# GpSimd normalises the probabilities of mixers A and B, with the scores of A and C two pairs ahead

## What is computed

```python
# A: windowed attention, 8 heads, with a sink logit
s = jnp.where(valid, s + bias, NEG)
p = jax.nn.softmax(jnp.concatenate([s, sink_l], axis=-1), axis=-1)[..., :-1]
o = jnp.einsum('bnkgqj,bnjkd->bnqkgd', p, vb)          # x silu(gate)
# B: latent attention, 4 heads, dense over all positions
s = jnp.einsum('bqhd,bkhd->bhqk', qb, k) * scale
p = jax.nn.softmax(s, axis=-1)
return jnp.einsum('bhqk,bkhd->bqhd', p, v)             # x silu(gate)
# C: 2-D neighbourhood attention, 4 heads
p = jax.nn.softmax(s.reshape(B, C_HEADS, GRID_W, kh * KW), axis=-1)
return layer_norm(DEEPNORM_ALPHA * x + concat([oa, ob, oc]) @ w_out, ln_g, ln_b)
```

## Time and profile before

| | us |
|---|---|
| median of 3 runs | 1917.07 (1913.8 to 1921.44) |
| the profiled execution, as timed | 1914.88 |
| its span, first to last instruction | 1913.1 |
| PE busy | 1821.9 (95%) |
| DVE busy | 940.6 (49%) |
| ACT busy | 786.1 (41%) |
| POOL busy | 467.6 (24%) |

### The profile page before, as it was taken

One profiled execution on the slowest core, in us unless ns is written; L12 is line 12 of the kernel. 1 busy time (PEld: TensorE's weight loads), 2 busy tenths in 40 slices (PEclk: granted clock), 3 DMA queues, 4 the chain that ended last, 5 costly groups with the idle time before them and its releaser, 6 DMA issues.

```text
span 1913.1 us, 32194 instructions
## 1 busy us (share of the span) xinstructions
PE 1821.9 (95%) x12530; PEld 1480.0 (77%) x12530; DVE 940.6 (49%) x2055; ACT 786.1 (41%) x1675; POOL 467.6 (24%) x683
## 2 busy tenths in 40 slices
PE   5999999999999999999999999999999999989996
PEld 3897578889886665889979866888898766578896
DVE  4466655311425765554453475460133277555626
ACT  3445643311225665452233365341212366644512
POOL 3453402311121362001242231140111125500113
PEclk9999999999999998999989999999999999999998
DMA  6865142211125020005146350621212062000312
GB/s 207 251 219 143 36 166 89 84 49 45 45 66 143 15 73 1 1 19 181 56 144 199 88 134 23 209 77 56 67 45 66 22 144 60 26 1 2 110 46 88
DMA packets 148165, 167.16 MB, mean 87 GB/s; under 512 B 18305, under 2 KB 134401, under 8 KB 147505
## 3 DMA queue, kind: packets, MB, share of 16 engines
q1 hardware_dynamic: 146080, 158.75, 27.9%
q0 software_dynamic: 1152, 4.19, 0.6%
q10 hardware_dynamic: 784, 2.16, 0.3%
HBM read 143.00 MB, written 32.65 MB: 92 GB/s over the span
## 4 chain that ended last, share of the span: by engine, by line
PE 88%; DVE 6%; ACT 3%; issue 1%; DMA 1%; POOL 0%; SPq 0%; DVEq 0%; ACTq 0%
PE psum L582 63%; PE psum L703 8%; PE psum L673 8%; PE psum L655 6%; DVE nmax L1056 2%; PE psum L592 1%; PE psum L714 1%; DVE pt_sb L1080 1%; DMA w_stage<-w_out 1%; DVE qB_lo L1217 1%; DMA qA<-x_prompt 0%; ACT w_hi L867 0%; POOL w_lo L473 0%; ACT qB_hi L962 0%; PE psum L568 0%
## 5 line engine op out<-in xcount | busy, mean ns | idle before, releaser
L582 PE MATMUL psum<-w_hi,x_hi 128*128 128x256 f32 (+1 forms) x1344 | 378.5, 282 | 11.5 <-DVE x_lo L1240 6.7
L582 PE MATMUL psum<-w_hi,x_lo 128*128 128x256 f32 (+1 forms) x1344 | 379.0, 282 | 0.0
L582 PE MATMUL psum<-w_lo,x_hi 128*128 128x256 f32 (+1 forms) x1344 | 377.5, 281 | 0.0
L582 PE MATMUL psum<-x_hi,w_hi 128*128 128x512 f32 x816 | 326.6, 400 | 2.4 <-DVE x_lo L1047 1.6
L582 PE MATMUL psum<-x_lo,w_hi 128*128 128x512 f32 x816 | 325.2, 399 | 0.0
L582 PE MATMUL psum<-x_hi,w_lo 128*128 128x512 f32 x816 | 324.9, 398 | 0.0
L473 POOL TENSOR_TENSOR w_lo<-w_stage,w_hi 128x1024 fp32r<-128x1024 f32 (+1 forms) x83 | 164.0, 1985 | 640.6 <-ACT w_hi L867 640.6
L473 DVE TENSOR_TENSOR w_lo<-w_stage,w_hi 128x1024 fp32r<-128x1024 f32 (+1 forms) x77 | 140.2, 1837 | 318.6 <-ACT w_hi L867 318.6
L582 PEld LDWEIGHTS psum<-w_hi,x_hi 128*128 128x128 f32 x1344 | 254.8, 190 | 13.2 <-issue 13.0
L582 PEld LDWEIGHTS psum<-w_lo,x_hi 128*128 128x128 f32 x1344 | 255.2, 190 | 0.2
L582 PEld LDWEIGHTS psum<-w_hi,x_lo 128*128 128x128 f32 x1344 | 253.5, 189 | 0.0
(11 more groups left out here) (141 smaller groups left out, 2678.9 us busy)
## 6 DMA issues: line engine op xcount, KB each, us to landing
w_stage<-w_in SPq DMA_DIRECT2D x48, 512.0 KB, 4.5
w_stage<-w_in SPq DMA_DIRECT2D x88, 256.0 KB, 3.4
toep<-rpb_tile SPq DMA_DIRECT2D x12, 1152.0 KB, 14.6
rpb_tile<-rpb_col SPq DMA_DIRECT2D x48, 192.0 KB
hT<-y SPq DMA_DIRECT2D x18, 512.0 KB, 11.2
y<-hT SPq DMA_DIRECT2D x18, 512.0 KB, 2.7
w_stage<-w_out SPq DMA_DIRECT2D x32, 256.0 KB, 4.2
w_stage<-w_out SPq DMA_DIRECT2D x16, 512.0 KB, 5.1
```

The source lines that it names most:

```text
L582: last = nc.tensor.matmul(out, w, x, start=(n == 0 and part != 1), stop=(n == len(pairs) - 1 and part != 0))
```

## The change

For A and B the group's division behind the values is taken out, and each unit's probabilities are divided ahead of the transpose: DVE takes one reciprocal for each unit (`unit_inverse`), POOL multiplies the probabilities by it in SBUF (`normalise`), in B with 1024 tokens once for each half, and T waits for POOL (`norm_done`) where it waited for ACT (`probs_done`). The gate is then multiplied by the outputs alone. C keeps what it had.

In phase AC the scores run two pairs ahead of T where they ran one pair ahead: PE's order is S of pair j+1, T of pair j-1, R for C, V of pair j-2, and DVE and ACT take the minimum and the exponential of unit i+2 at step i (`LEAD`). There are six probability slots for this, the sixth in a tensor of its own. PE's order in B stays, without R. In DVE's loop `unit_inverse` of unit k-1 stands behind `bound_scores` of unit k; in B, k is i.

```diff
@@ pe_steps
+    if ph == "AC":
+        for j in range(1, n + 2):
+            if EARLY <= 2 * j + 2 < 2 * n:
+                steps += [("S", 2 * j + 2), ("S", 2 * j + 3)]
+            if 0 <= j - 1 < n:
+                steps.append(("T", j - 1, 0))
+            if j - 2 >= 2 and (j - 2) % 2 == 0:
+                steps.append(("R", (j - 2) // 2 - 1))
+            if 0 <= j - 2 < n:
+                steps.append(("V", j - 2))
+        return steps + [("R", n // 2 - 1)]
...
-P_SLOTS = 5
+P_SLOTS = 6
+LEAD = 2
@@ PE, transpose_probs
-                    pe.wait_ge(probs_done, probs_no[s, u])
+                    if u[0] == "C":
+                        pe.wait_ge(probs_done, probs_no[s, u])
+                    else:
+                        pe.wait_ge(norm_done, norm_no[s, u, hf])
@@ PE, spread_sums
+                if units_of(ph, s)[4 * g][0] != "C":
+                    return
@@ ACT
-                        if (EARLY if ph == "AC" else 0) <= i < len(U):
-                            exp_unit(s, i, U[i])
-                act.wait_ge(values_done, s + 1)
+                        k = i + LEAD if ph == "AC" else i
+                        if (EARLY if ph == "AC" else 0) <= k < len(U):
+                            exp_unit(s, k, U[k])
+                wait_full(act, ("O", s, "B", NT - 1))
@@ DVE
+            def unit_inverse(s, u):
+                j = unit_index[s, u]
+                dve.wait_ge(probs_done, probs_no[s, u])
+                nc.vector.reciprocal(rinv[:, j:j + 1], psums[:, j:j + 1]).then_inc(inv_done, 1)
@@ DVE, the loop
-                    for i in range(len(U) + lag - 2):
-                        if (EARLY if ph == "AC" else 0) <= i < len(U):
-                            bound_scores(s, i, U[i])
+                    for i in range(-1 if ph == "AC" else 0, len(U) + lag - 2):
+                        k = i + LEAD if ph == "AC" else i
+                        if (EARLY if ph == "AC" else 0) <= k < len(U):
+                            bound_scores(s, k, U[k])
+                        if 0 <= k - 1 < len(U) and U[k - 1][0] != "C":
+                            unit_inverse(s, U[k - 1])
...
-                        if i >= 5 and (i - 5) % 4 == 0 and i - 5 < len(U):
+                        if i >= 5 and (i - 5) % 4 == 0 and i - 5 < len(U) and U[i - 5][0] == "C":
                             group_rinv(s, ph, (i - 5) // 4)
...
+                        if i >= lag - 2 and (i - lag + 2) % 4 == 0 and i - lag + 2 < len(U) and U[i - lag + 2][0] != "C":
+                            group_out(s, ph, (i - lag + 2) // 4)
@@ POOL
+                def normalise(u, p, hf, n):
+                    j = unit_index[s, u]
+                    pool.wait_ge(inv_done, inv_no[s, u])
+                    cols = slice(512 * hf, 512 * hf + n)
+                    nc.gpsimd.tensor_scalar(p[:, cols], p[:, cols], rinv[:, j:j + 1], None, ALU.mult).then_inc(norm_done, 1)
+
+                for i in range(EARLY):
+                    sink_column(i)
+                for i in range(LEAD, len(U) + 5):
+                    if EARLY <= i < len(U):
+                        (sink_column if U[i][0] == "A" else window_bias)(i)
+                    k = i - LEAD
+                    if 0 <= k < len(U) and U[k][0] == "A":
+                        normalise(U[k], p_slot(k), 0, key_tiles(U[k], s) * P)
...
-                for g in range(len(b_units(s)) // 4):
-                    spread_rinv(s, "B", g)
+                for i, u in enumerate(b_units(s)):
+                    for hf in range(len(halves_of(u, s))):
+                        normalise(u, pB[:, i % 3, :], hf, 512)
```

More of the change, by code:

```diff
@@ L194, in pe_steps @@
             steps.append(("V", j - late))
-    return steps + [("R", n // 2 - 1)]
+    return steps
 def dense_wide(ph, s):
@@ L302, in encoder_kernel, with p_slot @@
         kB_lo = [w[:, 1].rearrange("p k n -> p (k n)").rearrange("p (h n) -> p h n", h=2) for w in (w_hi, w_lo)]
-        pAC = w_stage[:, :, :, :].rearrange("p h k n -> p (h k n)")[:, 0:P_SLOTS * 385].rearrange("p (u n) -> p u n", n=385)
+        pAC = w_stage[:, :, :, :].rearrange("p h k n -> p (h k n)")[:, 0:5 * 385].rearrange("p (u n) -> p u n", n=385)
+        def p_slot(i):
+            return pAC[:, i % P_SLOTS, :] if i % P_SLOTS < 5 else pAC_last[:, :]
         t5_neg = hT[0:A_HEADS, 0, 0:512]
@@ L427, in encoder_kernel @@
         pt_dve_no = Numbered([(s, h) for s in range(RUNS) for ph in PHASES for h in halves(s, ph) if not copied_by_act(s, *h)])
-        group_no = Numbered(all_groups)
+        group_no = Numbered([(s, ph, g) for s, ph, g in all_groups if units_of(ph, s)[4 * g][0] == "C"])
+        inv_no = Numbered([(s, u) for s, u in all_units if u[0] != "C"])
+        norm_no = Numbered([(s, u, hf) for s, u in all_units if u[0] != "C" for hf in range(len(halves_of(u, s)))])
         xh_no = Numbered([("xT", s, t, i) for s in range(RUNS) for t in range(NTILES[s]) for i in range(2)])
@@ L704, in values @@
                                                     pt_sb[:, slot, (c % 4) * P:(c % 4 + 1) * P], start=(c == 0), stop=(c == nk - 1))
-                if ph == "B" and 2 * j + 2 == len(units_of(ph, s)):
-                    last.then_inc(values_done, 1)
+                if pair[0][0] != "C" and j % 2:
+                    last.then_inc(bank_full[b], 1)
             def spread_sums(s, ph, g):
+                if units_of(ph, s)[4 * g][0] != "C":
+                    return
                 b = uses["O", s, ph, g][0]
@@ L1066, in bound_scores @@
                         dve.wait_ge(biasA_loaded[t - 1], 16 * (s + 1))
-                    nc.vector.tensor_tensor_reduce(out=pAC[:, i % P_SLOTS, 0:n], in0=ps[:, 0:n], in1=reversed_keys(biasA[:, t - 1, kv, :] if t else biasA0[:, kv, :], k0, n),
+                    nc.vector.tensor_tensor_reduce(out=p_slot(i)[:, 0:n], in0=ps[:, 0:n], in1=reversed_keys(biasA[:, t - 1, kv, :] if t else biasA0[:, kv, :], k0, n),
                                                    scale=1.0, scalar=nsink[:, A_HEADS * (s // 2) + h:A_HEADS * (s // 2) + h + 1], op0=ALU.add, op1=ALU.min,
@@ L1102, in group_out @@
             def group_out(s, ph, g):
-                dve.wait_ge(gate_scaled, group_no[s, ph, g])
                 key = ("O", s, ph, g)
+                if units_of(ph, s)[4 * g][0] == "C":
+                    dve.wait_ge(gate_scaled, group_no[s, ph, g])
+                else:
+                    wait_full(dve, key)
+                    if g == 0:
+                        dve.wait_ge(silu_done, last_gate(s))
                 dst = gate_slice(s, ph, g)
@@ L1354, in window_bias @@
                                             reversed_keys(toep[:, slot, 3 * (h % 2) + WIN_TYPE[b], :], 0, n), ALU.add).then_inc(biasC_done, 1)
-                for i in range(-2, len(U) + 3):
-                    if i >= 6 and (i - 6) % 4 == 0:
-                        spread_rinv(s, "AC", (i - 6) // 4)
-                    if i + 2 < len(U):
-                        (sink_column if U[i + 2][0] == "A" else window_bias)(i + 2)
+                def normalise(u, p, hf, n):
[11 more added lines that the diff above has]
+                        normalise(U[k], p_slot(k), 0, key_tiles(U[k], s) * P)
+                    if i >= 8 and (i - 8) % 4 == 0 and U[i - 8][0] == "C":
+                        spread_rinv(s, "AC", (i - 8) // 4)
                 for t in range(NT):
```

24 lines of the change are left out of this document (10 added, 14 removed).

## The result

The changed kernel takes 2132.01 us (median of 4 runs, 2123.37 to 2135.11) against 1917.76, a ratio of 1.112 (95% interval 1.110 to 1.115). The profiled execution takes 2129.97 us with a span of 2128.1. The forecast was 1988, with a range of 1970 to 2022.

A forecast was written before the change was run, and what follows sets the result against it. PE was taken to bound every stretch. Costs of 89.4 us (63.6 + 19.3 + 1.7 + 4.8) less gains of 18.1 gave +71.3 us, so 1988 us against 1917.07, 3.7% slower, range 1970 to 2022.

The forecast's parts named there:

- PE's wait in B: Mixer B, T of each pair's second unit: 2.0 us wait with 1024 tokens, 1.38 us with 512.
- the new one has one tensor input and is nearest to the copy: POOL's division in A and B: 0.65 us for 512 columns, 0.50 for 384, 0.40 for 256.
- So PE stays the bound: Mixer A: POOL rises to 47 of 78.6 us, and A gains its 10.6 us but for the head.
- The rival that A gets a new bound: Mixer A: DVE becomes the bound by waiting for ACT, the 10.6 us are not gained, 1999 us; chance 0.05.
- the clock: Rival, mixer B: waits lower PE's clock, 4 us each time, 2028 to 2108 us; chance 0.08.
- the forecast's terms: Mixer B: costs 63.6 + 19.3 + 1.7 less 5.3 and 1.2, on 304.7, make 383 us.
- the wait's links: Mixer B, 1024 tokens: minimum 1.23, reciprocal 0.12, 0.06 to POOL, division 0.65, 0.08 to PE; 2.0 us wait.
- the 0.12 us ahead of DVE's copy: Mixer B, 1024 tokens: a reciprocal between minimum and DVE's copy makes V wait 0.12 us more per pair.
- the lead and the slots: Phase of A and C: the last T of C has its exponential a pair earlier, 0.25 us a run, 1 us gained.
- R worth its 10.6 us: Mixer A: R goes from PE's path for 48 groups at 0.22 us, 10.6 us gained.
- The head of A: Start of mixer A: first reciprocal stands behind the last gate's multiplication, 1.2 us lost in each of four runs, 4.8 us.
- the faster one: Rival, mixer B: the reciprocal comes before the next scores complete, no wait, only the head's loss remains, 1904 us; chance 0.04.

The follow-up runs named there:

- The run with A alone: The changed kernel with mixer B divided as in the kernel before and only mixer A divided on GpSimd: 1942.51 us, ratio 1.016.
- the cheaper form: The changed kernel with GpSimd's division written as a product of two tensors, the reciprocal broadcast along the row: 2038.95 us, ratio 1.065.
- the split: The changed kernel with B divided as before, A's even units on GpSimd, odd on ACT, first four reciprocals ahead of the last gate: 1906.9 us, ratio 0.9957.
- The run with the forecast's own prices: The changed kernel with GpSimd dividing only 144 of each 512 columns in B and 80 in A: 2022.67 us, ratio 1.058.
- the lead alone: The kernel before with only the scores two pairs ahead in A and C and six probability slots, divisions as before: 1911.92 us, ratio 0.9994.

## Why the prediction was wrong, step by step

Direction and place were right: slower, by PE's wait in B for the reciprocal behind the next minimum. The size was a third of the measured one, 71 us where 214 came, and the range ended 110 us short. Three steps made that, some 40, 40 and 69 us by the sums below; the projections, 6 us shorter, take a little back.

The first is the term "the new one has one tensor input and is nearest to the copy", 0.65 us. It was 1.563, and it lay outside the bounds too: the upper one, 1.345, came from a subtraction of two inputs, taken for dearer than anything with one. The runs show the reverse, since the same product written with two inputs takes 1.041. The Trainium skill (GPSIMD Engine Reference, section 3.1) has 0.77 us for 512 columns as a best case; neither form reaches it here, and the measurement decides. In B the term enters 44 times: (1.56 - 0.65) x 44 = 40 us.

The second follows in A, where POOL was put at 47 of 78.6 us, "So PE stays the bound". At 1.2 us for each of 64 divisions it has 75 us and 12 of sink columns, more than the stretch is long. The rival that A gets a new bound was there, but with DVE in the place of GpSimd. The run with A alone shows the loss, 30 us where a gain of some 7 was summed, and the cheaper form and the split, both with PE holding the chain in A again, show whose it is.

The third is the clock, a rival with a chance of 0.08, set against with "here 7 us of work stand around each". The run with the forecast's own prices went to 0.83 and spent 54 us more of PE's busy time at waits of 2.0 us, 37 us of B's length over the forecast's terms; filling the waits gave 46 us of B back in the changed kernel. With the waits at their true length (30 x 2.95, as a pair at the full clock takes 9.96 where it took 7.0; 14 x 2.3, some 3.5 for the last pairs, less 5.3 for R, 119 us) some 69 of B's 188 us remain for the clock; this split is worked out, the 46 are measured. The Trainium skill (TensorE: Matmul & The Clock Gate, HAM oscillation) names waits in each round of a loop as what re-throttles the engine, in an example with a DMA's waits, longer than these; the trace agrees, 0.65 to 0.82 in B.

What held: the wait's links (0.26 to the minimum, 1.23, then 0.08 and 0.08 where 0.12 and 0.06 were put, and 2.87 us in all with the true division); the 0.12 us ahead of DVE's copy (0.07 in the chain of the pairs at full clock); the lead and the slots as neutral; R worth its 10.6 us in A and C only where nothing replaces it as the bound (9.6 measured, 1.3 of them with the lead alone). The head of A was put at 4.8 us; with cheap divisions the phase takes 334.1 us and with the reciprocals ahead of the gate, and the split, 327.6, which leaves up to 6.5 for it. Of the rivals, the faster one (the wait is not there) did not come, since the minimum does stand ahead in DVE's order, as the forecast had read. What it describes, a reciprocal ahead of the minimum, was tested and brought back 149 of 214 us.

## What to carry to other kernels

When a step moves to the engine that seems idle, ask what stands ahead of it in that engine's and in its feeder's order, and whether that needs work which the waiting engine issued just before: here such a ring cost more than the work itself. An operation that the trace doesn't show needs a range that the nearest rows don't close, and where it is repeated for every unit its price times the count must be set against the stretch as a possible bound. And a wait of PE can be dearer than its length, as it was here: count the matmuls behind it at the lower clock as well.

## What the hardware showed

GpSimd's product of a tensor with one scalar for each partition (TENSOR_SCALAR, fp32) took 924, 1245 and 1563 ns for 256, 384 and 512 columns, 2.5 ns a column and 0.28 us at the start; as a product of two tensors, the scalar broadcast along the row, 614, 828 and 1041 ns, 1.67 ns a column. The form with one tensor input is the dearer one, by a half.

PE's granted clock fell to a mean of 0.82 in B when each pair had a wait of 2.9 us between transposes (pairs of 10.0 us at the full clock, up to 12.6 where it fell), and to 0.83 with waits of 2.0 us; with the waits filled by matmuls it was 0.97. Which part the transposes at the wait's edges have in this was not tried.
